# Five edits around the three attentions of a two-model stack on one core

## The reference

```
first_block: h += (sigmoid(..)*s5(u)@w + sigmoid(..)*sliding_window_attention(q,k,v)@w) @ w_out
             h += peer_mixer(rms_norm(h))          # 512 tokens x 128 gathered experts
second_block, for l in 0, 1:
  x += 0.5*swiglu(rms_norm_2(x))
  h = rms_norm_2(x)
  aq,ak,av,bq,bk,bv,cq,ckv,ckr = split(h @ w_in)
  oa = rms_norm_2(softmax(s1) @ v - lam * softmax(s2) @ v)     # a: 4 heads x 2 maps, 512 keys
  ob = banded softmax with a sink, 8 heads, 128-blocks, 2 or 3 key blocks each   # b
  oc = mla: rms_norm_2(cq) @ w_uq, rms_norm_2(ckv) @ w_ukv, 4 heads, 512 keys    # c
  mix = sum over a, b, c of sigmoid(h @ w_gate) * (o @ w_branch)
  x += mix @ w_out
  x += 0.5*swiglu(rms_norm_2(x))
```

## Time and profile before

| | before |
|---|---|
| median of 3 runs | 4780.8 us |
| profiled execution: its own time | 4776.13 us |
| profiled execution: span | 4773.9 us |
| PE busy | 4310.2 us, 90% |
| DVE busy | 2562.6 us, 54% |
| POOL busy | 1944.8 us, 41% |
| ACT busy | 1335.9 us, 28% |
| mean granted TensorE clock | 0.955 |

### The profile page before, as it was taken

How to read it: one execution, slowest core, us unless ns; L and a number is a source line. 1 busy time by engine, 2 the same in 40 slices (tenths; PEclk the granted TensorE clock), 3 DMA queues, 4 the chain that set the end, 5 groups by cost and what they waited for, 6 DMA issues and landing times.

```text
span 4773.9 us, 49892 instructions
## 1 busy us (share of the span) xinstructions
PE 4310.2 (90%) x15900; PEld 2887.4 (60%) x15900; DVE 2562.6 (54%) x4586; ACT 1335.9 (28%) x2892; POOL 1944.8 (41%) x1596
## 2 busy tenths in 40 slices
PE   7998988887778787899989999999999989999998
PEld 4565753333333333588856666888888756757887
DVE  6965676767667675543263535542442254336442
ACT  2223222222222222332132222332332132232322
POOL 4342443333333333444524243444444523344443
PEclk8999998989998999999999899999999999999999
DMA  5121169999999999423212121223223201112322
GB/s 133 44 71 49 67 260 422 421 421 421 421 411 421 412 421 419 159 97 95 95 35 71 40 69 60 97 96 94 97 95 95 84 32 62 53 58 71 106 94 82
DMA packets 161749, 806.07 MB, mean 169 GB/s; under 512 B 17617, under 2 KB 26241, under 8 KB 96001
## 3 DMA queue, kind: packets, MB, share of 16 engines
q0 software_dynamic: 73728, 536.90, 27.1%
q1 hardware_dynamic: 83104, 260.15, 16.4%
q10 hardware_dynamic: 4704, 6.42, 0.7%
HBM read 798.17 MB, written 5.24 MB: 168 GB/s over the span
## 4 chain that ended last, share of the span: by engine, by line
PE 67%; DMA 14%; DVE 11%; DVEq 3%; ACT 2%; issue 2%; POOL 0%; ACTq 0%; POOLq 0%
PE bank L638 17%; PE bank L639 16%; PE bank L640 16%; PE bank L945 7%; DMA rows_x<-in_peer_uv,expert 5%; DMA rows_o<-in_peer_uv,expert 4%; DMA rows_w<-in_peer_uv,expert 4%; PE bank L727 1%; DVE rows_x L1978 1%; PE bank L1036 1%; DVE hst L1756 1%; PE bank L1020 1%; DVE rows_w L1978 1%; DVE rows_o L1978 1%; PE bank L983 1%
## 5 line engine op out<-in xcount | busy, mean ns | idle before, releaser
L585 POOL TENSOR_TENSOR wl<-raw,wh 128x1024 fp32r<-128x1024 f32 (+3 forms) x320 | 746.1, 2332 | 853.6 <-ACT wh L1408 853.6
L638 PE MATMUL bank<-xh,wh 128*128 128x512 f32 x2496 | 1008.4, 404 | 2.5 <-DVE xl L1519 2.2
L639 PE MATMUL bank<-xl,wh 128*128 128x512 f32 x2496 | 983.1, 394 | 0.0
L640 PE MATMUL bank<-xh,wl 128*128 128x512 f32 x2496 | 982.3, 394 | 0.0
L638 PEld LDWEIGHTS bank<-xh,wh 128*128 128x128 f32 x2496 | 475.1, 190 | 183.0 <-issue 84.3
L1408 ACT ACTIVATE wh<-raw 128x1024 fp32r<-128x1024 f32 x320 | 338.0, 1057 | 805.4 <-PE bank L640 627.3
L640 PEld LDWEIGHTS bank<-xh,wl 128*128 128x128 f32 x2496 | 475.5, 190 | 101.9
L639 PEld LDWEIGHTS bank<-xl,wh 128*128 128x128 f32 x2496 | 476.4, 191 | 94.2 <-issue 1.4
L554 POOL TENSOR_TENSOR wl<-raw,wh 128x1024 fp32r<-128x1024 f32 (+2 forms) x226 | 460.2, 2036 | 33.2 <-issue 1.0
L945 PE MATMUL bank<-rows_x,diag 128*128 128x512 f32 x688 | 345.1, 660 | 88.6 <-ACT diag L1374 88.6
L945 PE MATMUL bank<-rows_o,diag 128*128 128x512 f32 x688 | 337.2, 647 | 92.2 <-ACT diag L1374 92.2
(11 more groups left out here) (372 smaller groups left out, 6643.4 us busy)
## 6 DMA issues: line engine op xcount, KB each, us to landing
raw<-in_w_l SPq DMA_DIRECT2D x320, 512.0 KB, 3.2
raw<-in_w SPq DMA_DIRECT2D x58, 512.0 KB, 3.2
raw<-in_w_l SPq DMA_DIRECT2D x64, 448.0 KB, 3.2
raw<-in_w_l SPq DMA_DIRECT2D x56, 256.0 KB, 2.6
raw<-in_w SPq DMA_DIRECT2D x16, 256.0 KB, 2.6
bias_scratch<-brow ACTq DMA_DIRECT2D x1, 3072.0 KB, 33.8
raw<-in_uq_l SPq DMA_DIRECT2D x16, 192.0 KB, 2.3
rows_o<-in_peer_uv,expert POOLq DMA_INDIRECT x172, 17.4
```

Of the source, the lines that this page charges most:

```text
L585: gp.tensor_tensor(wl[:, slot, 0:w], raw[:, rslot, 0:w], f32(wh[:, slot, 0:w]), ALU.subtract).then_inc(w_split.sem, 1)
L638: pe.matmul(bank[b][:], wh[:, slot, c], ah, start=k == 0, stop=False)
L639: pe.matmul(bank[b][:], wh[:, slot, c], al, start=False, stop=False)
L640: mm = pe.matmul(bank[b][:], wl[:, slot, c], ah, start=False, stop=k == last)
```

## The change

1. Summed banks first: in the first block's attention and in b, DVE's read of the bank `total` moves from the end of its step to the start. PE makes its share of the gate tile before the value products, not after.
2. Attention a: DVE normalises step s-1 before it takes the maxima of step s. The drain between bias and maxima stays in step 0 only.
3. The first three tiles of `in_b` become a stage `in_b0` of their own, ahead of `br_a`. POOL makes their high parts. PE does half of the first tile before the sums of squares of `batch`, the other half and two more after.
4. c: DVE adds the squares of each norm, so that PE sums two tiles with ones and not five, in the middle of the sixth `in_c` product. The rotary keys' second product and their sum are read between the two norms.
5. `branch("c")`: ACT makes the high part of `mix`, between its roundings of the weights of `out`. DVE takes the low part one tile later.

```diff
-    "in_a": whole(12, 8), "gate_a": whole(8, 8), "br_a": whole(8, 4),
-    "in_b": whole(7, 8), "gate_b": whole(8, 8), "br_b": whole(8, 4),
+    "in_a": whole(12, 8), "gate_a": whole(8, 8), "in_b0": whole(3, 8), "br_a": whole(8, 4),
+    "in_b": whole(4, 8), "gate_b": whole(8, 8), "br_b": whole(8, 4),
...
@@ PE, first block's attention (the same move in b, with share of gate_b)
+                if j < pairs:
+                    linear(AT_1["gate_a"], j // 4, None, normed, share=(j % 4, 4))
                 if j >= 3:
...
-                if j < pairs:
-                    linear(AT_1["gate_a"], j // 4, None, normed, share=(j % 4, 4))
...
@@ PE, end of attention a
                 pe.wait_ge(total_read.sem, total_read.at(use["total"], l))
+                linear(AT_L["in_b0"], 0, l, normed, share=(0, 2))
                 batch(BATCH_A, BANKS_A, l)
+                linear(AT_L["in_b0"], 0, l, normed, share=(1, 2))
+                for j in range(1, 3):
+                    linear(AT_L["in_b0"], j, l, normed)
...
@@ PE, before uq
-                for j in range(7):
+                for j in range(5):
                     linear(AT_L["in_c"], j, l, normed)
+                linear(AT_L["in_c"], 5, l, normed, share=(0, 2))
...
-                batch(BATCH_C, BANKS_C, l)
+                use.next("sq", 5)
+                for g, tiles_ in enumerate(BATCH_C):
+                    pe.wait_ge(group_added.sem, group_added.at(g + 1, l))
+                    pe.matmul(BANKS_C[g][:], ones[:], batch_work[tiles_[0]], start=True, stop=True).then_inc(group_sum.sem, 1)
+                linear(AT_L["in_c"], 5, l, normed, share=(1, 2))
+                linear(AT_L["in_c"], 6, l, normed)
...
@@ ACT, before the product out
+                for j in range(KD):
+
+                    act.wait_ge(mix_summed.sem, mix_summed.at(j + 1, l))
+                    act.activation(mixh[:, j, :], mix[:, j, :], ACT.Copy, scale=0.5).then_inc(mix_high.sem, 1)
+                    if j >= KD - RING:
+                        rounded(at_.tile0 + j - (KD - RING), l)
                 k = 0
                 for n in range(at_.tiles):
-                    rounded(at_.tile0 + n, l)
+                    if n >= RING:
+                        rounded(at_.tile0 + n, l)
...
@@ DVE, branch c
-                            dve.tensor_tensor(mix[:, j, :], mix[:, j, :], t_, ALU.add)
+                            ins = dve.tensor_tensor(mix[:, j, :], mix[:, j, :], t_, ALU.add)
                             if br == "c":
-                                settle()
-                                split(mix[:, j, :], mixh[:, j, :], mix_low(j), 0.5).then_inc(op_ready.sem, 1)
+                                ins.then_inc(mix_summed.sem, 1)
+                                if j > 0:
+                                    mix_rest(j - 1)
+                    if br == "c":
+                        mix_rest(KD - 1)
                     settle()
+
+                def mix_rest(j):
+
+                    dve.wait_ge(mix_high.sem, mix_high.at(j + 1, l))
+                    dve.scalar_tensor_tensor(mix_low(j), mix[:, j, :], 0.5, f32(mixh[:, j, :]), ALU.mult, ALU.subtract).then_inc(op_ready.sem, 1)
...
+                def add_squares(k):
+
+                    for g, tiles_ in enumerate(BATCH_C):
+                        if k not in tiles_:
+                            continue
+                        n = use.next("sq")
+                        if k > tiles_[0]:
+                            dve.wait_ge(sq_ready.sem, sq_ready.at(n, l))
+                            ins = dve.tensor_tensor(batch_work[tiles_[0]], batch_work[tiles_[0]], batch_work[k], ALU.add)
...
@@ DVE, attention a
-                        settle()
-                        rows_max(s, l, work[:, w0, :], T, w0, None, False)
-                        rows_max(s, l, work[:, w0 + 1, :], T, w0 + 1, None, True)
+                        if s == 0:
+                            settle()
...
+                    if s < 16:
+                        w0 = (2 * s) % 4
+                        rows_max(s, l, work[:, w0, :], T, w0, None, False)
+                        rows_max(s, l, work[:, w0 + 1, :], T, w0 + 1, None, True)
...
+                readout(AT_L["in_b0"], 0, l, scaled(qk[:, 0, :], 0.125))
+                use.next("sq", 4)
                 batch(BATCH_A, l, lambda k: oraw[:, k, :], lambda k: cs[:, 44:45], lambda k: oh[:, k, :], lambda k: ol[:, k, :])
+                for j in range(1, 3):
+                    readout(AT_L["in_b0"], j, l, scaled(qk[:, j, :], 0.125))
...
@@ DVE, attention b (the same move of L1858 in the first block)
                 for s in range(items_b + 4):
+                    if s >= 11 and (s - 11) % 8 == 0:
+                        head_out((s - 11) // 8)
...
-                    if s >= 11 and (s - 11) % 8 == 0:
-                        head_out((s - 11) // 8)
...
@@ DVE, c
+                readout(AT_L["in_c"], 5, l, lambda ps: dve.tensor_tensor(qk[:, 6, :], ps, rope_c[:], ALU.mult))
+                batch(BATCH_C[0:1], l, *c_parts)
+                readout(AT_L["in_c"], 6, l, lambda ps: dve.tensor_tensor(qk[:, 7, :], ps, rope_s[:], ALU.mult))
+                settle()
+                dve.tensor_tensor(qk[:, 6, :], qk[:, 6, :], qk[:, 7, :], ALU.add)
+                batch(BATCH_C[1:2], l, *c_parts)
```

More of the change, by code:

```diff
@@ L518, in _ @@
                     stage_l(f"gate_{br}", "w8_l")
+                    if br == "a":
+                        stage_l("in_b0", "w8_l")
                     stage_l(f"br_{br}", "w4_l")
@@ L600, in _ @@
                 n, hi = 0, FFN_HI
-                for s in ("in_a", "gate_a", "br_a", "in_b", "gate_b", "br_b", "in_c", "uq", "ukv", "gate_c", "br_c", "out"):
+                for s in ("in_a", "gate_a", "in_b0", "br_a", "in_b", "gate_b", "br_b", "in_c", "uq", "ukv", "gate_c", "br_c", "out"):
                     if s not in HI_STAGES:
@@ L1005, in _ @@
                     linear(AT_L["br_a"], j, l, pair(oh, ol), (xn_ready, a0))
-                for j in range(7):
+                for j in range(4):
                     linear(AT_L["in_b"], j, l, normed)
-                values(1, l, lambda f: vf[:, f, :], AT_L["in_b"], 6)
+                values(1, l, lambda f: vf[:, f, :], AT_L["in_b"], 3)
                 items_b = BH * NB
@@ L1026, in _ @@
                         turn_tile(work[:, i % 4, :], l, min(qb + 2, NB) - max(qb - 1, 0))
+                    if s < items_b:
+                        linear(AT_L["gate_b"], s // 4, l, normed, share=(s % 4, 4))
                     if s >= 3:
@@ L1040, in _ @@
                             mm.then_inc(summed.sem, 1)
-                    if s < items_b:
-                        linear(AT_L["gate_b"], s // 4, l, normed, share=(s % 4, 4))
                 t0 = use["total"] - 4
@@ L1551, in batch @@
                 use.next("xn", len(flat))
-                use.next("sq", len(flat))
-                for k in range(len(flat) + 1):
-                    if k < len(flat):
+                for n in range(len(flat) + 1):
+                    if n < len(flat):
+                        k = flat[n]
                         g = [k in tiles_ for tiles_ in norms].index(True)
@@ L1559, in batch @@
                         dve.scalar_tensor_tensor(full(k), full(k), gain(k), batch_work[norms[g][0]], ALU.mult, ALU.mult).then_inc(full_ready.sem, 1)
[L1560 to L1562 removed]
+                    if n >= 1:
+                        k = flat[n - 1]
+                        dve.wait_ge(hi_ready.sem, hi_ready.at(first + n, l))
+                        dve.tensor_tensor(lo(k), full(k), f32(hi(k)), ALU.subtract).then_inc(xn_ready.sem, 1)
                 settle()
@@ L1817, in _ @@
             for j in range(pairs + 4):
+                if j >= 7 and j % 4 == 3:
+                    dve.wait_ge(summed.sem, summed.at(use.next("total"), None))
+                    dve.tensor_copy(q1[:, (j - 7) // 4, :], total[:]).then_inc(total_read.sem, 1)
                 if j < pairs:
@@ L1854, in _ @@
                     ins.then_inc(prob_ready.sem, 1)
-                if j >= 7 and j % 4 == 3:
-                    dve.wait_ge(summed.sem, summed.at(use.next("total"), None))
-                    dve.tensor_copy(q1[:, (j - 7) // 4, :], total[:]).then_inc(total_read.sem, 1)
             settle()
```

33 lines of the change are left out of this document (17 added, 16 removed).

## The result

The changed kernel took 4613.4 us, the median of 4 runs (4610.7 to 4614.6), against 4782.0 us (4778.3 to 4785.4, 4 runs). The ratio is 0.9646, with a 95% interval of 0.9632 to 0.9660: 168.6 us less. The forecast was 4632 with a range of 4612 to 4682: the direction and nearly all mechanisms hold, but the time was put 19 us too high, and it lies only 1.4 us inside the range.

The account below looks back on a forecast made before the run. PE was busy 90% of the span, so gains must come from its idle or slow time. Terms of 32.7 + 39 + 28 + 16 + 19.5 + 10 = 145 us off 4776.1 gave 4631, forecast as 4632, range 4612 to 4682.

Parts of the forecast that it names:

- My main choice: All terms: price each PE wait by its disturbed stretch against an undisturbed one, giving more than the sum of waits.
- only idle time comes back: Rival, whole kernel: PE stays at the lower clock level as often, gain only the waits, 96 us, 4680; chance 0.07.
- Bank read first, first block: First block's attention: seven waits of 2.93 us for `total` vanish, steps 8.60 to 3.93 us; gain 32.7 us.
- Bank read first, b: Attention b: six waits for `total`, three a layer, vanish with their slow stretches; gain 39 us, bounds 28 and 41.
- Attention a: Loop of a: probabilities ready 1.37 us earlier, 15.4 us gained less 1.4 at the end; 28 us in both layers.
- the moved normalising is late: Rival, attention a: exponential not ready or POOL's splits hit the normalising; a gives nothing, 4659; chance 0.11.
- Three products ahead of `br_a`: Between a and b: products cover the norm chain, 14.11 us becomes 6.0; 8.1 us a layer, 16 in all.
- Squares of c: Before c: 14.56 us for 24 matmuls becomes 4.9; 9.7 us a layer, 19.5 in all, bounds 15 and 21.
- High part of `mix`: Behind c: DVE loses 8 instructions and a drain per layer, waits of 8.4 us and slow stretches; 10 us, bounds 3 and 13.
- Slower by the clock (4821): Rival, five loops of first block, a and b: denser load brings the lower clock, 190 us against 145 gained; chance 0.02.
- A stage that feeds the products becomes late: Rival, in b, before `br_a` or in `out`: 15 to 25 us less gain, 4651; chance 0.07.
- the change does little: Rival, whole kernel: each wait is replaced by one of its kind, gain under 10 us, 4770; chance 0.03.

Follow-up runs that it names:

- The last experiment: Changed kernel with four linears of b instead of three ahead of a's output, one whole ahead of a's last transposes: 4600.3 us, ratio 0.9618.

## Why the prediction was right, and where it was wrong

**Idle time costs more than itself.** My main choice, to price a wait by its disturbed stretch, is right, and it is now shown and not only read off: with PE kept busy in the same waits the three loops lose 29.6 us of their time. The rival "only idle time comes back" (4680) is out.

**Bank read first, first block: 32.7 forecast, 33.4 measured, partly by chance.** I took seven disturbed steps. Only six of 8.60 us lie between the first and last scores, and each went down to 4.03 in the variant with the older order on PE: 27.4 us. That variant gained 24.3 in the loop, since the first steps are longer than before (one of 7.38 us against 4.25). The changed kernel gained 31.4 there, because its order adds 7.1 us, which I had not forecast; 2.0 more came behind the last scores. My term took the order as free and the start of the loop as undisturbed, and the two mistakes of opposite sign nearly cancel: that it is right to 0.7 us is luck.

**Bank read first, b: 39 forecast, 53.1 measured. This is the step that failed.** I wrote "Two undisturbed steps are half of 13.74, 6.9 us", and took these steps as unchanged. They became shorter too: most by 0.2 us, and those of 4.14 us by some 0.57, as they no longer wait for probabilities. That is 6.9 us a layer and 13.8 us in all, which is the whole miss of 14.1. What I had priced, the six waits with their slow stretches, is 126.1 - 106.5 = 19.6 us a layer by the variant with the older order, so 39.3 for both: this part of the term is right to 1 us. The upper bound of 41 was wrong, since I bounded the edit by what a wait can give and did not look at the seams between groups on PE. The kernel before had the rows for it: the starts in a step show what follows each group, and by how much.

**Which half did it.** In b each half alone gains most: the read 19.6 us, PE's order 22.4 and 21.0 (126.1 - 103.7, 126.2 - 105.2), both 26.6. In the first block the read alone gains 24.3 us, the order alone 1.1, both 31.4. So the parts must not be added up: the order shortens the wait, and whether that brings anything is decided by the clock. The first block's 1.1 us is from one execution; the fastest of that variant was 12 us faster as a whole, and no trace shows where.

**Attention a: 28 forecast.** The loop gained 16.8 and 17.7 us where I had 15.4. Four steps came to 22.4 us, not to my 22.1. But I had counted one step in four as one that gains nothing, for its value products, and the first four of the 14 have none: they gained 6.9 us in layer 0 (26.6 to 19.7) where I had 4.4. In layer 1 it was the step ahead of these 14 that gained 1.5 us, which undoing the edit did not bring back. The tail was priced at 1.4 us of loss a layer; undoing the edit shows 1.8 in one layer and 0.2 in the other. By undoing it the edit is worth 34.2 us by the stretches (16.8 + 19.4 - 2.0). The rival "the moved normalising is late" (4659) is out. Its cover was thin, but it holds. The rows of a step of the changed kernel, POOL's first, then DVE's (the first of them from the step before):

```profile
2428.07 2.40 POOL L559 TENSOR_TENSOR wl<-raw,wh 128x1024 fp32r<-128x1024 f32 x1
```

```profile
2425.05 0.55 DVE L2157 TENSOR_SCALAR work<-work,stat,cs 128x512 f32<-128x512 f32 x1
...
2428.31 1.28 DVE L2146 SCALAR_TENSOR_TENSOR work<-dist_a,bank 128x512 f32<-128x512 f32 x2 [0.68 <-PE bank L988]
2429.51 0.15 DVE L2155 RECIPROCAL stat<-stat 128x2 f32<-128x2 f32 x1
2429.75 1.01 DVE L2157 TENSOR_SCALAR work<-work,stat,cs 128x512 f32<-128x512 f32 x1
2430.85 0.75 DVE L2159 SCALAR_TENSOR_TENSOR work<-work,stat 128x512 f32<-128x512 f32 x1
```

DVE waited 0.68 us for scores at the head of this step, and that slack takes up the 0.46 us by which L2157 is stretched here (0.55 us at 2425.05, without POOL). The reciprocal waits for no exponential.

**Three products ahead of `br_a`: 16 forecast, 13.1 measured** (13.6 by undoing it alone). The wait of 5.7 us is gone. Of the 19 matmuls that took 14.11 us in the earlier trace rows the eight sums now take 3.0 us, and eleven behind them 2.9, so the 8.1 us a layer that I had priced are there. But ahead of them stands the wait of 3.75 us at the end of a, and the value products behind that wait still run at the lower clock (L997, 6.28 us for eight; 5.16 in the kernel before). I had priced the new tail by its delay of 1.4 us alone and not looked at its clock. The last experiment takes it away and gains 13.8 us more at that place.

**Squares of c: 19.5 forecast, 15.5 measured.** The step that failed here is "4 passes at 0.43 and 14 at 0.23 are 4.9 us: 9.7 us a layer less". The wait of 5.0 us is gone and so are the slow products behind it. Against that PE waits 1.4 us instead of 0.6 in this stretch for POOL's low parts, a rival that I had named for other stages:

```profile
PE bank L643 <- POOL wl L590: 1.4, 4, 0.6
```

The view counts the idle time from the end of a matmul's pipeline. By the starts these pauses cost more: in layer 0 five of them are 0.52 to 0.97 us where 0.23 is undisturbed, 2.4 us in all, against one of 0.98 us before, 0.75. In layer 1 it is 2.2 us against 0.6. That is some 1.6 of the 2.0 us a layer that are missing; the other 0.4 stay open. The additions were not late: PE waited for none of them.

**High part of `mix`: 10 forecast, 13.7 measured**, just above the top of the bounds (13). The waits of 8.4 us are gone, and 5.3 us more. I had allowed 1.6 us for slow stretches behind four waits, by no row; by the measure of the earlier trace rows, 1.7 us behind each of four waits, the term would have been 8.4 + 6.8 = 15.2 us.

**Slower by the clock (4821)** fell: the mean granted clock is 0.968, and in both loops of b, where next to no wait is left, it is 1.00. "A stage that feeds the products becomes late" (4651) and "the change does little" (4770) fell too: PE waits in b for probabilities only twice, 0.5 us each, and all its waits for POOL's low parts (2.9 us) lie between b and c.

In sum the terms were off by +0.7, +3.6 (a and what follows it, 47.6 for 44), +14.1, -4.0 and +3.7, and by -0.9 for c and the rest: 17.2 us, from 145.2 to 162.4. The time was put 18.6 us too high (4632 for 4613.4): beside these 17.2 us, 1.1 are what I had added above the sum and 0.3 the difference between the profiled execution's gain and the median's. The 162.4 us lie just above the 162 to which my upper bounds add up, and 4613.4 lies below the 4615 to 4655 that I had given the forecast itself; b's miss would have put it further out had the squares of c not fallen 4 us short. That it is still in the range is in part luck.

**A reading to set right.** In the earlier trace rows I took the stretched L2115 as in agreement with the whole of the rule. Its start (2446.02) is 0.05 us ahead of POOL's cast (2446.07), and yet DVE's instruction is the longer one, 1.63 us, and the cast took its 1.03. The rows agree with the blocking, but that the one that starts first keeps the port they do not show.

## What to carry to other kernels

Read a loop's undisturbed step too, seam by seam: when an edit reorders an engine's groups, each step's length can change, and over 96 steps some 0.2 us each made 20.9 us here. Price a wait of PE by the length of its disturbed stretch and by the clock in it, and expect jumps: in the first block a wait cut from 2.9 to 2.1 us gained nothing in the profiled execution, in b one cut to 1.6 us cost only itself in five cases of six. Where a wait can't be removed, work that is needed anyway put into it (a later stage's product) gives back the clock as well, even if that work outlasts the wait.

## What the runs showed of the hardware

- Twelve matmuls of 128x512 that nobody reads, put into each of 13 PE waits of up to 3.0 us, made the program 31 us faster (ratio 0.9929, 0.9915 to 0.9942). The granted clock of the three loops with the waits went from 0.92, 0.89 and 0.89 to 0.99, 1.00 and 1.00, and they became 29.6 us shorter.
- A wait of 2.1 us at every fourth step of 3.8 us brought the clock down to 0.73 over two steps, more than one of 2.9 us did at the same steps (0.80 over the long step and 1.00 behind it, 382.90 to 395.43 in the kernel before). A wait of 1.6 us at every eighth step of b left it at 1.00 five times, and was followed by a step at 0.65 once. Three waits of 0.69 us ahead of c were followed by a step at 1.00, 0.82 or 0.58 in different kernels. How the chip decides is not settled by these runs.
- Value products with 64 stationary columns start 0.59 us after the start of four transposes of 128x128, linears 0.41 us after it. Whether the shape makes the difference, or the semaphores that the value products wait for, is not shown.
- DVE's operations beside POOL: the sum of two SBUF tiles of 128x512 took 0.76 to 1.95 us. The row group of the six:

```profile
L2103 DVE TENSOR_TENSOR work<-work x4: 762/1357/1951, 2674.4 to 4013.0; 128x512 f32<-128x512 f32 x4
L2103 DVE TENSOR_TENSOR work<-work,pt x2: 1140/1142/1144, 2684.5 to 4019.2; 128x512 f32<-128x512 f32 x2
```

The columns are the shortest, median and longest time in ns. The Trainium skill (SBUF — State Buffer, "Who interferes with whom") has an instruction with two SBUF inputs blocked by a POOL instruction that reads SBUF; these rows agree. At the start of the sum of 0.76 us a cast of POOL had 0.22 us to go, at those of 1.14 and 1.95 us a subtraction had 0.60 and 1.40 us to go, and in each case the sum ended 0.54 or 0.55 us after POOL's instruction. I had put the sums at 0.7 to 1.4 us. They lie under products of `in_c`, so the delay cost PE nothing.
